# Feed-forward norm: the first eight gate and up blocks on the scaled residual, the token factor after the product

## The reference, cut to what matters

```python
h_res = h_res + merged @ w_out[l]
h2 = rmsnorm(h_res, norm2_w[l])      # x * rsqrt(mean(x*x) + RMS_EPS) * w
gu = h2 @ w_gate_up[l]
h_res = h_res + (silu(gu[..., :D_FF]) * gu[..., D_FF:]) @ w_down[l]
```

## Time and profile before

| | |
|---|---|
| median of 3 runs | 1340.81 us (1338.44 to 1342.98) |
| the profiled execution | 1337.83 us, its span 1336.0 us |
| PE busy, share of the span | 1248.0 us, 93% |
| DVE, ACT, POOL | 857.3 us 64%, 629.6 us 47%, 217.6 us 16% |
| mean granted TensorE clock | 0.973 |

### The profile page before, as it was taken

One profiled execution on the slowest core, in us unless ns is written; L12 is line 12 of the kernel. 1 busy time (PEld: TensorE's weight loads), 2 busy tenths in 40 slices (PEclk: granted clock), 3 DMA queues, 4 the chain that ended last, 5 costly groups with the idle time before them and its releaser, 6 DMA issues.

```text
span 1336.0 us, 26909 instructions
## 1 busy us (share of the span) xinstructions
PE 1248.0 (93%) x11228; PEld 1200.2 (90%) x11228; DVE 857.3 (64%) x1369; ACT 629.6 (47%) x1014; POOL 217.6 (16%) x237
## 2 busy tenths in 40 slices
PE   5999999998899999997898999999998897999997
PEld 5889999998899989986798889899998897999997
DVE  4755756666668567664588686786876565555544
ACT  6644455443545454425478623333333625444443
POOL 3100140011101400030000172452632000000000
PEclk9999999999999999988899999999999988999999
DMA  6553554444545544444264322323323553555653
GB/s 247 189 198 120 185 160 139 147 155 132 194 153 172 178 127 144 148 152 139 95 198 142 123 89 92 108 69 96 92 85 100 168 191 114 170 184 183 197 195 110
DMA packets 59912, 196.34 MB, mean 147 GB/s; under 512 B 6382, under 2 KB 14088, under 8 KB 59664
## 3 DMA queue, kind: packets, MB, share of 16 engines
q1 hardware_dynamic: 49248, 179.33, 42.1%
q10 hardware_dynamic: 10016, 12.90, 2.8%
q0 software_dynamic: 528, 2.40, 0.7%
HBM read 190.37 MB, written 4.23 MB: 146 GB/s over the span
## 4 chain that ended last, share of the span: by engine, by line
PE 76%; DVE 9%; ACT 7%; issue 4%; DVEq 2%; POOLq 1%; DMA 0%; ACTq 0%; POOL 0%
PE stream_ps L288 16%; PE stream_ps L289 15%; PE stream_ps L303 12%; PE stream_ps L282 4%; ACT w_hi L268 3%; DVE w_lo L274 3%; PE stream_ps L284 3%; PE stream_ps L283 3%; PE free_ps L1853 2%; PE free_ps L1841 2%; PE stream_ps L1925 2%; PE stream_ps L339 1%; PE stream_ps L344 1%; PE stream_ps L340 1%; PE stream_ps L1683 1%
## 5 line engine op out<-in xcount | busy, mean ns | idle before, releaser
L274 DVE TENSOR_TENSOR w_lo<-raw,w_hi 128x1024 fp32r<-128x1024 f32 x342 | 429.6, 1264 | 265.9 <-ACT w_hi L268 262.7
L288 PE MATMUL stream_ps<-h_hi,w_hi 128*128 128x256 f32 (+1 forms) x1504 | 382.7, 291 | 24.9 <-DVE h_lo L1227 14.4
L268 ACT ACTIVATE w_hi<-raw 128x1024 fp32r<-128x1024 f32 x342 | 356.5, 1052 | 52.3 <-PE stream_ps L1683 26.2
L289 PE MATMUL stream_ps<-h_lo,w_hi 128*128 128x256 f32 (+1 forms) x1504 | 375.9, 286 | 0.0
L288 PEld LDWEIGHTS stream_ps<-h_hi,w_hi 128*128 128x128 f32 x1504 | 290.5, 193 | 32.9 <-issue 22.4
L289 PEld LDWEIGHTS stream_ps<-h_lo,w_hi 128*128 128x128 f32 x1504 | 291.0, 194 | 0.2
L303 PE MATMUL stream_ps<-h_hi,w_lo 128*128 128x256 f32 (+1 forms) x1424 | 200.0, 283 | 3.0 <-DVE w_lo L274 3.0
L303 PEld LDWEIGHTS stream_ps<-h_hi,w_lo 128*128 128x128 f32 x1424 | 183.3, 190 | 3.4 <-DVE w_lo L274 3.4
L282 PE MATMUL stream_ps<-h_hi,w_hi 128*128 128x256 f32 (+1 forms) x384 | 119.7, 312 | 2.1 <-DVE w_lo L274 2.1
L284 PE MATMUL stream_ps<-h_hi,w_lo 128*128 128x256 f32 (+1 forms) x384 | 108.5, 283 | 0.0
L283 PE MATMUL stream_ps<-h_lo,w_hi 128*128 128x256 f32 (+1 forms) x384 | 108.4, 282 | 0.0
(11 more groups left out here) (352 smaller groups left out, 2198.5 us busy)
## 6 DMA issues: line engine op xcount, KB each, us to landing
raw<-stream_dram SPq DMA_DIRECT2D x342, 512.0 KB, 3.6
gate_spill<-gate_out ACTq DMA_DIRECT2D x16, 128.0 KB, 2.8
decay<-gate_spill POOLq DMA_DIRECT2D x2, 640.0 KB, 8.0
xT<-xT_dram ACTq DMA_DIRECT2D x4, 272.0 KB, 7.8
wik<-wik_dram ACTq DMA_DIRECT2D x2, 544.0 KB, 5.1
mem_raw<-memT_dram ACTq DMA_DIRECT2D x2, 512.0 KB, 9.1
hankel<-rel_scratch POOLq DMA_DIRECT2D x1, 1024.0 KB, 8.6
x_spill<-xT ACTq DMA_DIRECT2D x1, 1024.0 KB, 4.8
```

The costliest lines, as they stand in the source:

```text
L268: nc.scalar.activation(w_hi[s][:, :, :], raw[:, s, :].rearrange("p (k n) -> p k n", k=KT), ACT.Copy).then_inc(hi_ready, 1)
L274: nc.vector.tensor_tensor(w_lo[s][:, :, :], raw[:, s, :].rearrange("p (k n) -> p k n", k=KT), w_hi[s][:, :, :].bitcast(F32), ALU.subtract) ...
L288: nc.tensor.matmul(ps, l_hi, r_hi, start=first, stop=False)
L289: nc.tensor.matmul(ps, l_hi, r_lo, start=False, stop=False)
```

## The change

In the out projection ScalarE, before each square, also writes `ys_hi` = gain x residual rounded, and VectorE writes `ys_lo` one block later. GpSimd adds the eight squares into one tile, and TensorE's sum is one matmul behind the first two gate/up blocks. Gate/up blocks 0 to 7 (`EARLY = 2` groups of four) run on `ys_hi` and `ys_lo`. For these VectorE multiplies each product by `rstd`: the gate product before ScalarE's Silu (new semaphore `pre_ready`), the up product before it is multiplied with the Silu. The scaled `oT` is written behind block 3, its halves are split in the places of blocks 4, 5 and 7, and from block 8 on everything is as before, on `hS_hi` and `hS_lo`. `f_act` and `f_val` move in memory to lie ahead of `f_hi`.

```diff
@@ GpSimd, at the end of its queue
+            add_squares(pool, wideS, sq_ready, 16 + 8 * LAYERS, sqsum_ready)
@@ ScalarE
                         ahead(split_hi, act, G + w, s)
-                        act.wait_ge(dve_evac, SLOTS + D_at + 4 * w + s + 1)
+                        n = 4 * w + s
+                        act.wait_ge(dve_evac, SLOTS + D_at + n + 1)
+                        nc.scalar.activation(ys_hi[:, n, :], xS[:, n, :], ACT.Copy, scale=gain_col(G_NORM2)(n)).then_inc(vhi_ready, 1)
                         act.wait_ge(mlo_ready, 4 * LAYERS + 2)
...
             squares(G_WO, D2 + 32)
-            rstd_of(act, 2 + LAYERS, S)
-            split_norm_hi(2 * LAYERS + 4, hS_hi, oS)
             for w in range(0, FT // 2):
                 for s in range(SLOTS):
-                    ahead(split_hi, act, G_GU + w, s)
-                    if s % 2 == 0:
+                    if (w, s) != (0, 1):
+                        ahead(split_hi, act, G_GU + w, s)
+                    if (w, s) == (0, 0):
+                        ahead(split_hi, act, G_GU, 1)
+                        rstd_of(act, 2 + LAYERS, S)
+                    if w == 1 and s < 2:
+                        norm2_hi(s)
+                    if w < EARLY and s % 2 == 0:
+                        act.wait_ge(pre_ready, 2 * w + s // 2 + 1)
+                        nc.scalar.activation(f_act[:, s // 2, :], f_act[:, s // 2, :], ACT.Silu).then_inc(fact_ready, 1)
+                    elif s % 2 == 0:
@@ VectorE
                     nc.vector.tensor_tensor(xt, stream_ps[s][:, 0:S], xt, ALU.add).then_inc(dve_evac, 1)
-            split_norm(2 + LAYERS, G_NORM2, 2 * LAYERS + 2, oS, xS, hS_hi, hS_lo)
+                    if 4 * w + s:
+                        raw_norm2_lo(4 * w + s - 1)
+            raw_norm2_lo(KT - 1)
+            for s in range(2):
+                ahead(split_lo, dve, G_GU, s)
+            dve.wait_ge(rstd_ready, 3 + LAYERS)
             for w in range(0, FT // 2):
                 for s in range(SLOTS):
-                    ahead(split_lo, dve, G_GU + w, s)
+                    if w or s >= 2:
+                        ahead(split_lo, dve, G_GU + w, s)
+                    if w < EARLY and s % 2 == 0:
+                        dve.wait_ge(blk_done, SLOTS + 4 * (G_GU + w) + s + 1)
+                        nc.vector.tensor_tensor(f_act[:, s // 2, :], stream_ps[s][:, 0:S], rstd[:, 0:S], ALU.mult).then_inc(pre_ready, 1)
                     if s % 2 == 1:
                         f = bass.ds(2 * w + s // 2, 1)
                         dve.wait_ge(blk_done, SLOTS + 4 * (G_GU + w) + s + 1)
+                        if w < EARLY:
+                            nc.vector.tensor_tensor(f_val[:, s // 2, :], stream_ps[s][:, 0:S], rstd[:, 0:S], ALU.mult)
+                            nc.vector.drain()
+                            dve.wait_ge(fact_ready, 2 * w + s // 2 + 1)
+                            nc.vector.tensor_tensor(f_val[:, s // 2, :], f_val[:, s // 2, :], f_act[:, s // 2, :], ALU.mult).then_inc(dve_evac, 2)
...
+                    if (w, s) == (0, 3):
+                        for half in range(2):
+                            scale_rows(dve, oS, xS, gain_col(G_NORM2), half, n32_ready)
+                    if w == 1 and s in (1, 3):
+                        norm2_lo(s // 2)
@@ TensorE
-            sum_squares(pe, wideS, 16 + 8 * LAYERS)
-            first_blocks(pe, G_GU, dve_evac, D2 + 41, hS_hi, hS_lo, (nlo_ready, 2 * LAYERS + 3))
...
+            first_blocks(pe, G_GU, dve_evac, D2 + 41, ys_hi, ys_lo, (vlo_ready, 1), KT)
+            pe.wait_ge(sqsum_ready, 1 + LAYERS)
+            nc.tensor.matmul(free_ps[0][:, 0:S], ones, wideS[:, 0, :], start=True, stop=True).then_inc(ss_ready, 1)
+            for w in range(FT // 2):
+                for s in range(0 if w else AHEAD, SLOTS):
+                    if w < EARLY:
+                        block_cols(pe, G_GU + w, s, dve_evac, D2 + 40 + 4 * w + s + 1, ys_hi, ys_lo)
+                    else:
+                        block_cols(pe, G_GU + w, s, dve_evac, D2 + 40 + 4 * w + s + 1, hS_hi, hS_lo,
+                                   (nlo_ready, 2 * LAYERS + 3) if (w, s) == (EARLY, 0) else None)
```

More of the change, by code:

```diff
@@ L56 @@
 FT = 22
+EARLY = 2
 C2_COLS = 6 * P + 13 * C
@@ L192, in build @@
                 yd_hi, yd_lo, ys_hi, ys_lo = (sb(n, [P, KT, S], F32R, br2) for n in ("yd_hi", "yd_lo", "ys_hi", "ys_lo"))
+            f_act, f_val = (sb(n, [P, 2, S], scope=two) for n in ("f_act", "f_val"))
             f_hi = sb("f_hi", [P, FT, S], F32R, two)
             f_lo = sb("f_lo", [P, FT, S], F32R, two)
-            f_act, f_val = (sb(n, [P, 2, S], scope=two) for n in ("f_act", "f_val"))
         h32p = oT
@@ L255, in build @@
         fact_ready, fhi_ready, flo_ready = (sem(n) for n in ("fact_ready", "fhi_ready", "flo_ready"))
+        vhi_ready, vlo_ready, pre_ready = (sem(n) for n in ("vhi_ready", "vlo_ready", "pre_ready"))
         held = sem("held")
@@ L940, in squares, with norm2_hi @@
                         ahead(split_hi, act, G + w, s)
-                        act.wait_ge(dve_evac, SLOTS + D_at + 4 * w + s + 1)
+                        n = 4 * w + s
+                        act.wait_ge(dve_evac, SLOTS + D_at + n + 1)
+                        nc.scalar.activation(ys_hi[:, n, :], xS[:, n, :], ACT.Copy, scale=gain_col(G_NORM2)(n)).then_inc(vhi_ready, 1)
                         act.wait_ge(mlo_ready, 4 * LAYERS + 2)
-                        nc.scalar.activation(wideS[:, bass.ds(4 * w + s, 1), :], xS[:, bass.ds(4 * w + s, 1), :],
-                                             ACT.Square).then_inc(sq_ready, 1)
+                        nc.scalar.activation(wideS[:, n, :], xS[:, n, :], ACT.Square).then_inc(sq_ready, 1)
+            def norm2_hi(half):
+                act.wait_ge(n32_ready, 2 * LAYERS + 4 + half + 1)
+                ks = slice(4 * half, 4 * half + 4)
+                nc.scalar.activation(hS_hi[:, ks, :], oS[:, ks, :], ACT.Copy).then_inc(nhi_ready, 1)
             squares(G_WO, D2 + 32)
-            rstd_of(act, 2 + LAYERS, S)
-            split_norm_hi(2 * LAYERS + 4, hS_hi, oS)
             for w in range(0, FT // 2):
                 for s in range(SLOTS):
-                    ahead(split_hi, act, G_GU + w, s)
-                    if s % 2 == 0:
+                    if (w, s) != (0, 1):
[9 more added lines that the diff above has]
+                    elif s % 2 == 0:
                         act.wait_ge(blk_done, SLOTS + 4 * (G_GU + w) + s + 1)
@@ L1471, in _, with raw_norm2_lo, norm2_lo @@
                                                op0=ALU.mult, op1=ALU.subtract).then_inc(mlo_ready, 1)
+            def raw_norm2_lo(k):
+                dve.wait_ge(vhi_ready, k + 1)
+                nc.vector.scalar_tensor_tensor(out=ys_lo[:, k, :], in0=xS[:, k, :], scalar=gain_col(G_NORM2)(k),
+                                               in1=ys_hi[:, k, :].bitcast(F32), op0=ALU.mult, op1=ALU.subtract).then_inc(vlo_ready, 1)
+            def norm2_lo(half):
+                dve.wait_ge(nhi_ready, 2 * LAYERS + 2 + half + 1)
+                ks = slice(4 * half, 4 * half + 4)
+                nc.vector.tensor_tensor(hS_lo[:, ks, :], oS[:, ks, :], hS_hi[:, ks, :].bitcast(F32), ALU.subtract).then_inc(nlo_ready, 1)
             dve.wait_ge(x_back, 16)
@@ L1485, in _ @@
                         dve.wait_ge(blk_done, SLOTS + 4 * (G_GU + w) + s + 1)
-                        dve.wait_ge(fact_ready, 2 * w + s // 2 + 1)
-                        nc.vector.tensor_tensor(f_val[:, s // 2, :], stream_ps[s][:, 0:S], f_act[:, s // 2, :], ALU.mult).then_inc(dve_evac, 2)
+                        if w < EARLY:
[4 more added lines that the diff above has]
+                        else:
+                            dve.wait_ge(fact_ready, 2 * w + s // 2 + 1)
+                            nc.vector.tensor_tensor(f_val[:, s // 2, :], stream_ps[s][:, 0:S], f_act[:, s // 2, :], ALU.mult).then_inc(dve_evac, 2)
                         dve.wait_ge(fhi_ready, 2 * w + s // 2 + 1)
```

## The result

The changed kernel is slower: 1344.5 us median against 1338.4 for the kernel before, ratio 1.0045 with a 95% interval of 1.0032 to 1.0058, +6.0 us (4.3 to 7.8). One of the twelve runs of the kernel before, of 1532 us, counts as slow and is left out of these numbers. The forecast was +5.6 us, 1346.4 on the median of 1340.8 that was known then.

A forecast was written before the change was run, and what follows sets the result against it. TensorE, busy 93% of the span, was taken to bound the kernel. Block 9 starting 3.2 us later plus 2.4 us of slow clock gave +5.6 us, 1346.4 on the median of 1340.81; range 1341.5 to 1349.5.

The forecast's parts named there:

- The ring in the out projection: Out projection: ys_hi joins the residual, square, weight-split loop; residuals 3.39 us apart instead of 2.99, residual 7 2.8 us later.
- Blocks 0 and 1, rstd: Gate/up start: block 2 6.18 us after residual 7, 8.2 us earlier than before; VectorE uses rstd 8.84 us after residual 7.
- the slow spell in block 1: Gate/up block 1: TensorE's clock 0.79 over 8 us, 1.7 us of full speed lost, expected in the new kernel too.
- GpSimd: Sign of a wrong forecast: block 2 much later than 1131.8 if GpSimd's adds of the squares hold the sum up.
- The way from rstd to the second half of hS_lo: Gate/up blocks 2 to 8: VectorE and ScalarE alternate; block 8 stands 6.1 us, block 9 starts 3.2 us later than before.
- The clock: Behind block 8's idle stretch: slow TensorE matmuls cost 2.4 us, from nothing to 2.7 at most.
- The sum: End of the kernel: +3.2 and +2.4 give +5.6 us, 1346.4 on the median; chance 0.60.
- The Silu table: Gate/up start: Silu's table load comes into the chain right behind Exp, at 1.28 us, without the skill's further drain.
- The gain did not stay: Rival for gate/up: the chain does not bind, block 9 starts 8.2 us early, 1332.6; chance 0.12 for gain in part or whole.
- The case without a slow spell: Rival for block 8: the chain binds but no slow spell follows the stop, +1.5 to +3.2 us, about 1343.5; chance 0.22.
- The worse case: Rival for gate/up: Silu table costs beyond its load, slow clock in blocks 4 to 7 reaches the chain, +7 to +8; chance 0.06.

The follow-up runs named there:

- the ring alone: The kernel before with ys_hi and ys_lo written in the out projection as in the change, read by nobody: ratio 1.0029, +3.9 us.
- the norm's steps taken out: The changed kernel without scaled rows, halves of hS_hi and hS_lo and block 8's wait for them: ratio 0.9962 to the kernel before.
- the squares later: The changed kernel with ScalarE's ys_hi and square of residual n moved behind the split of block n+3: ratio 0.9982 to the kernel before.
- products first: The changed kernel reordered in gate/up blocks 0 to 7, VectorE multiplying by rstd before splitting a weight block: ratio 0.9945 to the kernel before.

## Why the prediction was right, point by point

- *The ring in the out projection.* 3.39 us a block, residual 7 23.76 us behind residual 0, forecast 23.75. Shown by itself by the ring alone.
- *Blocks 0 and 1, rstd.* Residual 7 to block 2: 1132.80 - 1125.47 = 7.33, forecast 6.18. The mechanism was right and the size off: the slow spell in block 1 was longer (0.62 mean clock over the 8 us, 0.79 in the earlier trace rows). It was not GpSimd, which the forecast named for this case: its last add was over at 1127.5, 5 us before block 2. VectorE used rstd 9.99 us behind residual 7 and not 8.84, so everything behind it came 1.1 us later than worked out. Of the five kernels with this stop one had the short spell (7.3 us from block 1 to block 2, with the norm's steps taken out), the changed kernel and three others the long one (8.4).
- *The way from rstd to the second half of hS_lo.* 25.8 us, forecast 25.4; TensorE goes on 1.28 behind its start, forecast 1.3. The links held to a few hundredths, up to 0.1. The stops in us, with the forecast in brackets: block 4 0.3 (0.6), block 6 1.67 (1.9), block 8 5.79 (6.1).
- *The clock.* 2.5 us: block 8's last 16 matmuls and block 9 took 1169.73 - 1162.52 = 7.2 us instead of 1.9 + 2.84. Forecast 2.4. Filling the stop takes these 2.4 us away. That the value was met to 0.1 is luck: behind the same stop of 5.79 us the kernel with the squares later lost 1.4. Slow matmuls also ran in block 7, behind block 6's stops, and cost nothing, since block 7 was done 4 us before VectorE took its product (1155.5 and 1159.43).
- *The sum.* 5.6 by the forecast, 7.15 in the traces, 6.0 in the medians. The trace's surplus is the 1.1 of the first spell and 0.4 of the way. The ratio's interval, +4.3 to +7.8, holds both, so the medians' nearness to the forecast says little. The level of 1346.4 was 1.9 too high, since the three runs known then had a median 2.4 above that of the eleven runs here.
- *The Silu table.* It came into the chain as forecast, at its load's price only. ScalarE's timeline of the changed kernel, Exp, load, Silu:
```profile
1135.01 0.42 ACT L375 ACTIVATE rstd<-rstd 128x256 f32<-128x256 f32 x1
1135.44 1.28 ACT L969 ACT_TABLE_LOAD   x1
1136.74 0.42 ACT L969 ACTIVATE f_act<-f_act 128x256 f32<-128x256 f32 x1
```
  The load starts 0.01 us behind Exp's end, and Silu 0.02 behind the load. The Trainium skill, "ScalarE: Activation LUTs", What ACT_TABLE_LOAD costs, gives 1.28 us for the load, and the trace agrees; its further drain of 1.38 us is not there, neither here nor in the earlier trace rows.
- *The rivals.* The gain did not stay, since the way, with the last 1.3 us to TensorE, was 27.1 and not 15.3 us; with products first it is 15.8, and the gain stays but for 0.6 us (X is 6.5 us under before, and block 2 was 7.1 us ahead). The case without a slow spell is refuted by the windows. The worse case isn't what happened either, though the traces' 7.15 us reach its size: the Silu table cost its load alone, and the slow matmuls in block 7 did not reach the chain.

## What to carry to other kernels

When work is taken off the main engine's path, write down the queues of the engines that take it over, step by step, and look for a step that waits for the other engine between two splits or loads: each adds a round trip, and the round trips of a stage have to fit in the main engine's time for it. Here a way of 25.8 us beside the 17 us of blocks 2 to 7 lost 6 us; the same steps in an order that puts the products first took 14.5 and gained 7. A part of the same kernel that already does the same thing is the best ruler: its distances carried over to a few tenths of a microsecond, except for the slow spell in them, which was 1.1 us longer here.

## What the runs showed of the hardware

The length of a slow spell behind the same idle stretch (2.9 us) differs between executions: mean clock 0.79 or 0.62 over 8 us, 1.1 us of difference up to block 2. Behind the stop of 5.79 us it was 7.21 us to block 10 in the changed kernel and 6.17 us with the squares later. Filling that stop with unused matmuls kept the granted clock at 1.00 and took 2.4 us out of what follows it, in the one execution traced. I had not expected how far profiled executions differ ahead of the changed stretch: in the ten kernels that are alike up to there the out projection began between 1091.8 and 1098.9 us, and 7 us is more than the 6.0 that the change costs. A comparison of two traces has to be made from a point just ahead of the change.
